# RWKV stage of a two-block transformer kernel: the state's products of y move into the scan over chunks, and the 128-row products follow behind it

## The chip, the cores and the metric

The program runs on one core of a Trainium2 chip. The metric is device time in microseconds (us) of one launch, all weights read from HBM. TensorE (PE) multiplies matrices into PSUM, VectorE (DVE) and ScalarE (ACT) read PSUM and write SBUF, GpSimd (POOL) and SyncE (SP) here mostly issue DMAs. The engines run side by side and are ordered by semaphores alone.

## The reference, cut to what matters

The first block has a mixer with two halves, an attention and an RWKV-7 layer, and a conv FFN; the second block (two layers) follows. The change is inside the RWKV layer, whose core is a scan over the 512 tokens, for 8 heads of 64 channels:

```
def step(state, inp):                       # state: heads x 64 x 64
    sa = einsum('bhvk,bhk->bhv', state, a_t)
    state = state * w_t + sa[..., None] * b_t + v_t[..., None] * k_t
    return state, einsum('bhvk,bhk->bhv', state, r_t)   # y_t
```

The kernel computes it in 8 chunks of 64 tokens. Within a chunk everything is a triangular matrix product; between chunks only the 64x64 state is handed on. For a chunk c, y is a sum of three products: the state at the chunk's start by r (the *state's product*), the corrected values U by the masked scores of b and r (the TR product), and v by the masked scores of k and r (the MR product).

## The kernel before, in words

The work stands in this order: input norm, projections of the mixer, the attention, the RWKV projections, then the RWKV stage (about 390 to 728 us of the span), the merge of both halves (L2017), the output product, and then the FFNs and the second block, which are long rows of 128x128 by 128x512 products in split precision (L1598 to L1600) and fill the other three quarters of the span.

The RWKV stage treats the 8 heads in 4 pairs (p = 0 to 3). Head hb = 0 of a pair sits on partitions 0 to 63, head hb = 1 on 64 to 127, so a slice hd of 64 partitions picks a head. A tile t (of 4) is 128 tokens, that is two chunks. The order on each engine is written out by hand: the lists RW_PE, RW_ACT and RW_DVE (L78 to L106) name every step, each step increments its engine's semaphore once, and `took(p, name)` and `made(p, name)` on TensorE wait for a ScalarE or a VectorE step of that name. Steps with a "+" belong to the next pair and are laid between those of this pair.

For one pair TensorE does: scores (L1846), five levels of a triangular inversion (L1937, L1943, L1948, with ScalarE and VectorE between them), MV, U0 and WT (L1957, L1962, L1966), then the scan over the 8 chunks (L1971 to L1988). In chunk c it multiplies WT with the state Sh[c] (step u, L1977); VectorE adds U0 and writes U (L1356); TensorE adds the chunk's two contributions to the new state in PSUM (L1983, which needs no wait, and L1987, behind U); VectorE scales and adds them into Sh[c+1] (L1362), which the next chunk's u waits for. After the scan comes step y (L1989 to L2001): it waits for the last U, and then for each head and each tile t writes the TR product (L1995), the MR product (L1996) and two state's products (L1999, one for each chunk of 64 tokens) into bank 7 of PSUM, one head's four tiles after the other's. ScalarE copies bank 7 to tA (L760); TensorE transposes the next pair's A (tokA, L1898) meanwhile, and then forms the mean of y (L2004), and the rest of the pair's normalization and the next pair's scores follow. Sh keeps the states of all 8 chunks in SBUF, and AR (or a stage slot for odd pairs) keeps r.

Every operand in this stage is 32-bit float, and each product written in the code is two MATMUL and two LDWEIGHTS in the trace. In the trace's rows a shape such as 128*64 is the rows and columns of the PE array that the product uses: the TR and MR products use all 128 rows and 64 columns (columns 0 to 63 for head 0, 64 to 127 for head 1), the state's products use a quadrant, 64 rows and 64 columns.

Of the kernel before, what the change touches and what calls it, by code (L numbers as in the profile page):

```python
# [23 lines left out]
P = 128  # L24
S = 512
TT = S // P
# [10 lines left out]
HD = 64  # L37
# [6 lines left out]
CHUNK = 64  # L44
# [73 lines left out]
def upto(steps, name):  # L118

    return steps.index(name) + 1  # L120
# [29 lines left out]
def build(nc, A, out, first_block=True, second_block=True):  # L150
# [3 lines left out]
    with ExitStack() as ctx:  # L154
# [46 lines left out]
        psum = ctx.enter_context(nc.psum_tensor("psum", [P, 8, S], F32))  # L201
# [81 lines left out]
        if first_block:  # L283
# [34 lines left out]
            ARs = [AR[:], odd_ar.rearrange("p (t a n) -> p t a n", t=TT, a=2)]  # L318
# [1269 lines left out]
        def _(pe):  # L1588
# [90 lines left out]
            for k in range(KD):  # L1679
# [3 lines left out]
                for tt in range(TT):  # L1683
                    m = pe.transpose(psum[:, k % 4, tt * P:(tt + 1) * P], x_tok[:, tt, k * P:(k + 1) * P], ident)
# [4 lines left out]
            if first_block:  # L1689
# [13 lines left out]
                def made(name):  # L1703
                    pe.wait_ge(ns_dve, upto(NS_DVE, name))
# [25 lines left out]
                for n in range(6):  # L1730
                    took(f"sq{n}")
                    for t in range(TT):
                        c = 8 + 8 * n + 2 * t
                        last = pe.matmul(psum[:, 7, c:c + 2], raw_n[:, n % 2, t * P:(t + 1) * P], head_of,
                                         start=True, stop=True)
# [10 lines left out]
                for n in range(6):  # L1746
# [4 lines left out]
                    for t in range(TT):  # L1751
                        last = pe.transpose(psum[:, 4 + n % 2, t * P:(t + 1) * P], rexp_n[:, n % 2, t], ident)
# [12 lines left out]
                for j in range(TT):  # L1765
                    for h in range(NSA_HEADS):
                        rows = slice(HD * (h % 2), HD * (h % 2) + HD)
                        c = 32 * (h // 2)
                        last = pe.matmul(psum[:, 2 * j + h % 2, c:c + NC], q_n[rows, h // 2, j * P:(j + 1) * P],
                                         kcd[rows, h // 4, 0:NC], start=True, stop=True)  # L1770
# [22 lines left out]
                for m in range(M + 2):  # L1793
                    if m < M:
# [4 lines left out]
                        for c in range(2):  # L1799
                            last = pe.matmul(psum[:, 2 * (m % 2) + c, 0:(j + 1) * P], q_n[rows, h // 2, j * P:(j + 1) * P],  # L1800
                                             kd[rows, c, h // 4, 0:(j + 1) * P], start=True, stop=True)
                        last.then_inc(nscore_done, 1)
                    if m >= 2:
# [6 lines left out]
                        for c in range(2):  # L1810
                            for kt in range(j + 1):
                                last = pe.transpose(psum[:, 4 + c, kt * P:(kt + 1) * P],
                                                    Pn[:, g % 2, c, kt * P:(kt + 1) * P], ident)
# [16 lines left out]
                def rw(p, name, last):  # L1830

                    assert RW_PE[rw_count[0]] == (name, p), (name, p, RW_PE[rw_count[0]])
                    rw_count[0] += 1
                    last.then_inc(rw_pe, 1)
# [77 lines left out]
                for p in range(PAIRS):  # L1912
# [42 lines left out]
                    for m in range(8):  # L1955
                        t, hd = m % 4, slice(HD * (m // 4), HD * (m // 4) + HD)
                        last = pe.matmul(psum[:, 0, HD * m:HD * m + HD], MR[:, m, 0:P], tok[:, 3, t, hd], start=True, stop=True)  # L1957
# [3 lines left out]
                    for m in range(8):  # L1961
                        last = pe.matmul(psum[:, 1, HD * m:HD * m + HD], XT[:, m], MV[:, HD * m:HD * m + HD], start=True, stop=True)  # L1962
                    rw(p, "U0", last)
                    for m in range(8):
                        t, hd = m % 4, slice(HD * (m // 4), HD * (m // 4) + HD)
                        last = pe.matmul(psum[hd, 2, t * P:(t + 1) * P], tok[:, 0, t, hd], XT[:, m], start=True, stop=True)  # L1966
# [3 lines left out]
                    Ut = Ap[:, 4:8].rearrange("p m n -> p (m n)").rearrange("p (h t d) -> p h t d", h=2, t=TT)  # L1970
                    for c in range(NCH):  # L1971
                        t, q = c // 2, slice(CHUNK * (c % 2), CHUNK * (c % 2) + CHUNK)
                        if c >= 1:
                            made(p, f"S{c - 1}")
                        for hb in range(2):
                            hd = slice(HD * hb, HD * hb + HD)
                            last = pe.matmul(psum[q, 3 + hb, 0:HD], WT[hd, CHUNK * c:CHUNK * c + CHUNK], Sh[hd, c],  # L1977
                                             start=True, stop=True)
                        rw(p, f"u{c}", last)
                        if c < NCH - 1:  # L1980
                            for hb in range(2):
                                hd = slice(HD * hb, HD * hb + HD)
                                pe.matmul(psum[hd, 5 + c % 2, 0:HD], tok[q, 2, t, hd], tok[q, 3, t, hd], start=True, stop=False)  # L1983
                            made(p, f"U{c}")
                            for hb in range(2):
                                hd = slice(HD * hb, HD * hb + HD)
                                last = pe.matmul(psum[hd, 5 + c % 2, 0:HD], tok[q, 1, t, hd], Ut[q, hb, t], start=False, stop=True)  # L1987
                            rw(p, f"s{c}", last)  # L1988
                    made(p, f"U{NCH - 1}")  # L1989
                    for hb in range(2):  # L1990
                        hd = slice(HD * hb, HD * hb + HD)
                        for t in range(TT):
                            m = 4 * hb + t
                            dst = psum[hd, 7, t * P:(t + 1) * P]
                            pe.matmul(dst, Ut[:, hb, t], TR[:, m, P:2 * P], start=True, stop=False)  # L1995
                            pe.matmul(dst, tok[:, 3, t, hd], MR[:, m, P:2 * P], start=False, stop=False)  # L1996
                            for q in range(2):
                                part = psum[hd, 7, t * P + CHUNK * q:t * P + CHUNK * q + CHUNK]
                                last = pe.matmul(part, Sh[hd, 2 * t + q], ARs[p % 2][hd, t, 1, CHUNK * q:CHUNK * q + CHUNK],  # L1999
                                                 start=False, stop=q == 1)  # L2000
                    rw(p, "y", last)  # L2001
                    head(p + 1, "tokA")
                    took(p, "y")
# [3 lines left out]
                    for t in range(TT):  # L2007
                        last = pe.matmul(psum[:, 1, 2 * t:2 * t + 2], tB[:, t * P:(t + 1) * P], head_of, start=True, stop=True)
# [3 lines left out]
                    for t in range(TT):  # L2012
                        last = pe.transpose(psum[:, 1, t * P:(t + 1) * P], X[:, t], ident)
# [34 lines left out]
            if second_block:  # L2048
# [25 lines left out]
                for n in range(25):  # L2074
# [7 lines left out]
                    if n >= 1:  # L2082
                        m = n - 1
# [5 lines left out]
                        if m < 8:  # L2089
                            for tt in range(TT):  # L2090
                                last = pe.transpose(psum[:, 4 + m % 2, tt * P:(tt + 1) * P],
                                                    raw[:, m % 2, tt * P:(tt + 1) * P], ident)
                        else:
                            last = pe.matmul(psum[:, 4 + m % 2, :], perm, raw[:, m % 2], start=True, stop=True)
# [17 lines left out]
                for m in range(M + 2):  # L2112
                    if m < M:
# [3 lines left out]
                        for c in range(2):  # L2117
                            rows = slice(HD * c, HD * c + HD)
                            last = pe.matmul(psum[:, 2 * (m % 2) + c, :], q_t[rows, h, j * P:(j + 1) * P],
                                             k_t[rows, h, :], start=True, stop=True)  # L2120
                        last.then_inc(score_done, 1)
                    if m >= 2:
# [4 lines left out]
                        for kt in range(TT):  # L2127
                            last = pe.transpose(psum[:, 4 + g % 2, kt * P:(kt + 1) * P],
                                                E[:, g % 2, 0, kt * P:(kt + 1) * P], ident)
# [5 lines left out]
                for h in range(DIFF_HEADS):  # L2135
                    pe.wait_ge(osq_done, h + 1)
                    for tt in range(TT):
                        last = pe.matmul(psum[:, 4, 4 * h + tt:4 * h + tt + 1], norm_t[:, h % 2, tt * P:(tt + 1) * P],
                                         ones[:, 0:1], start=True, stop=True)
                    last.then_inc(ossq_done, 1)  # L2140
                for h in range(DIFF_HEADS):
# [3 lines left out]
                    for tt in range(TT):  # L2145
                        last = pe.transpose(psum[:, 5 + h % 2, tt * P:(tt + 1) * P], rexp[:, h % 2, tt], ident)
# [10 lines left out]
            for k in range(KD):  # L2157
# [3 lines left out]
                for tt in range(TT):  # L2161
                    m = pe.transpose(psum[:, k % 4, tt * P:(tt + 1) * P], y_out[:, k % 2, tt * P:(tt + 1) * P], ident)
# [120 lines left out]
```

## Time and profile before

| | us |
|---|---|
| runs (3) | 3217.89, 3223.37, 3224.57; median 3223.37 |
| span of the profiled execution, first to last instruction | 3221.2 |
| TensorE busy in it | 3039.4 (94%) |
| VectorE busy | 1522.2 (47%) |
| ScalarE busy | 980.2 (30%) |
| mean granted TensorE clock | 0.938 |

The page states no time of the profiled execution but its span; the median of the runs is 2.2 us above it. Busy time is the time in which at least one of an engine's instructions was under way. The granted clock is TensorE's clock as a share of 2.4 GHz; it takes two values, 1.00 and 0.50 (1.2 GHz), and a figure between them is a mean over a stretch.

### The profile page before, as it was taken

To read this page: it belongs to the slowest core of one execution; us is meant where nothing else is said; L and a number is where in the kernel's file an instruction comes from. 1 tells how busy PE (TensorE), PEld (TensorE's weight loads), DVE (VectorE), ACT (ScalarE), POOL (GpSimd) and SP (SyncE) were. 2 spreads that over 40 slices of the span, in tenths; PEclk is the share of its full clock that TensorE was granted. 3 is DMA by queue.
4 is the path that set the end of the run, shared out by engine and by line. 5 is a ranking of instruction groups with operands and counts; after the bars stand their busy time and mean duration, and the time that the engine had idled before them with its cause. 6 is when DMAs were issued, how large, how long until landed. Compare 5 with 4: busy or idle time off the path is not lost.

```text
span 3221.2 us, 36308 instructions
## 1 busy us (share of the span) xinstructions
PE 3039.4 (94%) x13935; PEld 2401.9 (75%) x13935; DVE 1522.2 (47%) x2198; ACT 980.2 (30%) x1520; POOL 88.2 (3%) x159
## 2 busy tenths in 40 slices
PE   7989888889999999999988999999999999999998
PEld 6844667767878878788866888878887763778887
DVE  4355744426667754555435333243322469343322
ACT  3344333323333322322223222232222216332222
POOL 0000000001100000001100000000000000000000
PEclk9679977779999999999997999999999999899999
DMA  6101400006632346455622333323323220123331
GB/s 216 52 1 44 149 1 1 1 1 200 221 110 96 96 125 189 147 192 188 193 73 73 94 97 93 91 85 98 95 87 99 79 79 1 40 85 98 96 90 63
DMA packets 89888, 309.15 MB, mean 96 GB/s; under 512 B 10288, under 2 KB 14000, under 8 KB 89648
## 3 DMA queue, kind: packets, MB, share of 16 engines
q1 hardware_dynamic: 69040, 232.07, 23.0%
q0 software_dynamic: 20736, 75.51, 7.5%
q8 instruction: 80, 1.31, 0.2%
q14 instruction: 32, 0.26, 0.0%
HBM read 305.44 MB, written 2.10 MB: 95 GB/s over the span
## 4 chain that ended last, share of the span: by engine, by line
PE 88%; DVE 8%; ACT 2%; issue 1%; DMA 0%; SPq 0%; DVEq 0%; ACTq 0%
PE psum L1598 23%; PE psum L1600 23%; PE psum L1599 23%; PE psum L1606 2%; PE psum L1800 1%; PE psum L1937 1%; PE psum L1943 1%; PE psum L1788 1%; PE psum L1740 1%; PE psum L1650 1%; PE psum L1646 1%; PE psum L1647 1%; DVE nmax L1533 1%; PE psum L1995 1%; PE psum L1999 1%
## 5 line engine op out<-in xcount | busy, mean ns | idle before, releaser
L897 DVE TENSOR_TENSOR w_lo<-stage,w_hi 128x1024 fp32r<-128x1024 f32 (+3 forms) x445 | 519.5, 1168 | 896.3 <-ACT w_hi L494 894.9
L1598 PE MATMUL psum<-h_hi,w_hi 128*128 128x512 f32 x2248 | 887.7, 395 | 13.9 <-POOL h_lo L479 10.1
L1600 PE MATMUL psum<-h_hi,w_lo 128*128 128x512 f32 x2248 | 879.0, 391 | 0.0
L1599 PE MATMUL psum<-h_lo,w_hi 128*128 128x512 f32 x2248 | 878.9, 391 | 0.0
L494 ACT ACTIVATE w_hi<-stage 128x1024 fp32r<-128x1024 f32 (+3 forms) x445 | 450.3, 1012 | 1332.9 <-PE psum L1600 1309.3
L1598 PEld LDWEIGHTS psum<-h_hi,w_hi 128*128 128x128 f32 x2248 | 423.9, 189 | 108.2 <-POOL h_lo L479 10.5
L1599 PEld LDWEIGHTS psum<-h_lo,w_hi 128*128 128x128 f32 x2248 | 424.0, 189 | 91.3 <-issue 3.4
L1600 PEld LDWEIGHTS psum<-h_hi,w_lo 128*128 128x128 f32 x2248 | 423.7, 188 | 89.8
L1598 PE MATMUL psum<-hid_hi,w_hi 128*128 128x512 f32 x880 | 351.3, 399 | 6.5 <-DVE hid L984 6.5
L1599 PE MATMUL psum<-hid_lo,w_hi 128*128 128x512 f32 x880 | 348.3, 396 | 0.0
L1600 PE MATMUL psum<-hid_hi,w_lo 128*128 128x512 f32 x880 | 348.2, 396 | 0.0
L1598 PEld LDWEIGHTS psum<-hid_hi,w_hi 128*128 128x128 f32 x880 | 165.5, 188 | 47.6 <-DVE hid L984 8.7
L1600 PEld LDWEIGHTS psum<-hid_hi,w_lo 128*128 128x128 f32 x880 | 165.2, 188 | 40.5
L1599 PEld LDWEIGHTS psum<-hid_lo,w_hi 128*128 128x128 f32 x880 | 165.5, 188 | 38.8
L984 DVE TENSOR_TENSOR hid<-s_buf,psum 128x512 f32<-128x512 f32 x88 | 60.5, 688 | 266.5 <-PE psum L1600 264.9
L935 DVE CUSTOM_DVE_ANT_0 mod_w<-mod_w,c_act 128x1024 f32<-128x1024 f32 x144 | 175.6, 1219 | 0.0
L469 POOL DMA_DIRECT2D mod_w<-in_mod_w x144 | 76.3, 530 | 1544.3 <-DVE modv L935 1367.1
L542 ACT ACTIVATE hid_hi<-hid 128x512 f32 (+1 forms) x110 | 67.9, 618 | 54.8 <-DVE hid L984 54.8
L503 ACT ACTIVATE norm_t<-xT 128x512 f32<-128x512 f32 x64 | 40.3, 630 | 133.1 <-DVE xT L1008 122.7
L1606 PEld LDWEIGHTS psum<-cst,norm_t 128*128 128x128 f32 x512 | 71.8, 209 | 11.1 <-ACT norm_t L503 6.7
L991 DVE TENSOR_TENSOR hid_lo<-hid,hid_hi 128x512 f32 (+1 forms) x110 | 75.3, 685 | 0.0
L1606 PE MATMUL psum<-cst,norm_t 128*128 128x1 f32 x512 | 67.4, 255 | 6.1 <-ACT norm_t L503 6.1
(363 smaller groups left out, 2842.8 us busy)
## 6 DMA issues: line engine op xcount, KB each, us to landing
stage<-in_up SPq DMA_DIRECT2D x220, 512.0 KB, 3.5
mod_w<-in_mod_w POOLq DMA_DIRECT2D x144, 512.0 KB, 4.1
stage<-in_down SPq DMA_DIRECT2D x80, 448.0 KB, 3.3
stage<-in_down SPq DMA_DIRECT2D x40, 512.0 KB, 3.6
stage<-in_w_in SPq DMA_DIRECT2D x24, 512.0 KB, 4.4
stage<-in_w_qkv SPq DMA_DIRECT2D x24, 512.0 KB, 3.5
stage<-in_w_merge SPq DMA_DIRECT2D x16, 512.0 KB, 4.5
PTn<-in_cmp_w SPq DMA_DIRECT2D x1, 4096.0 KB, 12.1
```

Of the source, the lines that this page charges most:

```text
L469: pool.dma_start(mod_w[:, e], A["mod_w"][bass.ds(t + e, 1)].rearrange("a p n -> (a p) n")).then_inc(mod_in[e], 16)
L494: act.activation(w_hi[:, c % 2, 0:kt * cols], stage[:, c % NSTAGE, 0:kt * cols], ACT.Copy).then_inc(hi_done, 1)
L503: act.activation(sq(n_norm, k), xT[:, k], ACT.Square).then_inc(sq_done, 1)
L542: act.activation(hid_hi[:, bass.ds(2 * i + q, 1), :].rearrange("p a n -> p (a n)"), hid[:, q], ACT.Copy).then_inc(hidhi_done, 1)
L897: dve.tensor_tensor(w_lo[:, c % 2, 0:kt * cols], stage[:, c % NSTAGE, 0:kt * cols], w_hi[:, c % 2, 0:kt * cols].bitcast(F32), ALU.subtract ...
L935: dve.tensor_tensor_reduce(out=mod_w[:, t % 2], in0=mod_w[:, t % 2], in1=c_act[:], scale=1.0, scalar=0.0, op0=ALU.mult, op1=ALU.add, accum ...
L984: dve.tensor_tensor(hid[:, q], s_buf[:, q], taps[:, 1] if f == 0 else bank(s.tile + 2 * q + 1), ALU.mult).then_inc(hid_done, 1)
L991: dve.tensor_tensor(hid_lo[:, tile, :].rearrange("p a n -> p (a n)"), hid[:, q], hid_hi[:, tile, :].rearrange("p a n -> p (a n)").bitcast( ...
L1598: pe.matmul(dst, wh[:, n], a_hi[:, k], start=start and n == 0, stop=False)
L1599: pe.matmul(dst, wh[:, n], a_lo[:, k], start=False, stop=False)
L1600: m = pe.matmul(dst, wl[:, n], a_hi[:, k], start=False, stop=stop and n == kt - 1)
L1606: m = pe.matmul(psum[:, 4, tt:tt + 1], sq(n_norm, k)[:, tt * P:(tt + 1) * P], ones[:, 0:1], start=(k == 0 and tt == 0), stop=(k == KD - 1) ...
```

## The change

The state's product of chunk c is issued inside the scan, behind that chunk's contributions to the state, both heads one after the other. It is the first to write bank 7 (`start` only for c = 0). Behind the scan only the MR and TR products are left; they run over the tiles outside and the heads inside, the MR product first, and add to what the scan left. Waits, steps and the semaphore of step y are the same in number and name, and so is the count of products.

```
@@ after step s{c}, in the loop over c
+                        for hb in range(2):
+                            hd = slice(HD * hb, HD * hb + HD)
+                            pe.matmul(psum[hd, 7, CHUNK * c:CHUNK * c + CHUNK], Sh[hd, c],
+                                      ARs[p % 2][hd, t, 1, CHUNK * (c % 2):CHUNK * (c % 2) + CHUNK], start=c == 0, stop=False,
+                                      skip_group_check=True)
                     made(p, f"U{NCH - 1}")
-                    for hb in range(2):
-                        hd = slice(HD * hb, HD * hb + HD)
-                        for t in range(TT):
-                            m = 4 * hb + t
+                    for t in range(TT):
+                        for hb in range(2):
+                            m, hd = 4 * hb + t, slice(HD * hb, HD * hb + HD)
                             dst = psum[hd, 7, t * P:(t + 1) * P]
-                            pe.matmul(dst, Ut[:, hb, t], TR[:, m, P:2 * P], start=True, stop=False)
-                            pe.matmul(dst, tok[:, 3, t, hd], MR[:, m, P:2 * P], start=False, stop=False)
-                            for q in range(2):
-                                part = psum[hd, 7, t * P + CHUNK * q:t * P + CHUNK * q + CHUNK]
-                                last = pe.matmul(part, Sh[hd, 2 * t + q], ARs[p % 2][hd, t, 1, CHUNK * q:CHUNK * q + CHUNK],
-                                                 start=False, stop=q == 1)
+                            pe.matmul(dst, tok[:, 3, t, hd], MR[:, m, P:2 * P], start=False, stop=False,
+                                      skip_group_check=True)
+                            last = pe.matmul(dst, Ut[:, hb, t], TR[:, m, P:2 * P], start=False, stop=t == TT - 1,
+                                             skip_group_check=True)
                     rw(p, "y", last)
```

## Rows read from the trace of the kernel before

**Rows 1.** The page: busy time of the engines, and the chain that ended last.

```profile
PE 3039.4 (94%) x13935; PEld 2401.9 (75%) x13935; DVE 1522.2 (47%) x2198; ACT 980.2 (30%) x1520; POOL 88.2 (3%) x159
...
PE 88%; DVE 8%; ACT 2%; issue 1%; DMA 0%; SPq 0%; DVEq 0%; ACTq 0%
```

**Rows 2.** The chain of 380 to 760 us, summed by line.

```profile
by line: PE psum L1937 10.5%; PE psum L1943 8.3%; PE psum L1995 5.3%; PE psum L1999 5.2%; PE psum L1977 4.1%; PE psum L1846 4.0%; PE psum L1987 3.6%; PE psum L1996 3.6%; issue 3.5%; PE psum L1598 3.3%; DVE XT L1340 3.3%; PE psum L1599 3.3%;
```

**Rows 3.** Timeline: start us, length us, engine, line, tile, count [idle before, releaser]; pair 0.

```profile
466.76 0.48 PE L1977 MATMUL psum<-Sh,Ap 64*64 64x64 f32 x4 [0.46 <-DVE Sh L1362]
...
467.63 0.69 PE L1995 MATMUL psum<-TR,Ap 128*64 128x128 f32 x2 [0.39 <-DVE Ap L1356]
...
468.11 0.63 PE L1996 MATMUL psum<-MR,tok 128*64 128x128 f32 x2
468.67 0.50 PEld L1999 LDWEIGHTS psum<-AR,Sh 64*64 64x64 f32 x4 [0.33 <-issue]
...
469.29 0.69 PE L1995 MATMUL psum<-TR,Ap 128*64 128x128 f32 x2
...
480.30 0.69 PE L1999 MATMUL psum<-AR,Sh 64*64 64x64 f32 x4
480.91 1.11 PE L1898 MATMUL psum<-cst,stage 128*128 128x128 f32 x4
```

**Rows 4.** Timeline of pair 3: the first and the last products of step y.

```profile
705.48 0.69 PE L1995 MATMUL psum<-TR,Ap 128*64 128x128 f32 x2 [0.39 <-DVE Ap L1356]
...
718.15 0.69 PE L1999 MATMUL psum<-stage,Sh 64*64 64x64 f32 x4
```

**Rows 5.** Windows: stretch, its length, PE busy (instructions), granted clock, DMA share, GB/s.

```profile
467.60:481.00 13.40, 13.37 (x65) 0.50 0.00 0
481.00:484.40 3.40, 3.40 (x11) 0.50 0.00 0
484.40:528.70 44.30, 41.31 (x298) 1.00 0.01 1
...
560.90:562.90 2.00, 2.00 (x7) 0.50 0.00 0
...
640.80:644.80 4.00, 4.00 (x14) 0.50 0.00 0
...
658.50:685.70 27.20, 24.57 (x202) 1.00 0.01 1
...
728.00:733.60 5.60, 5.54 (x13) 0.50 0.52 151
```

**Rows 6.** The same products grouped by line over 380 to 760 us: busy, mean ns.

```profile
L1996 PE MATMUL psum<-MR,tok 128*64 128x128 f32 x64 | 20.3, 421 | 0.0
```

**Rows 7.** Timeline of step WT in pair 3: whole, at 688.95, and at 689.80 us.

```profile
688.35 2.88 PE L1966 MATMUL psum<-XT,tok 128*64 128x128 f32 x16
...
688.62 0.63 PE L1966 MATMUL psum<-XT,tok 128*64 128x128 f32 x2
...
689.47 0.70 PE L1966 MATMUL psum<-XT,tok 128*64 128x128 f32 x4
```

**Rows 8.** Timeline of the scan: a chunk's end at the low clock, and one at the full clock.

```profile
465.82 0.48 PE L1987 MATMUL psum<-Ap,tok 64*64 64x64 f32 x4 [0.17 <-DVE Ap L1356]
466.42 0.28 DVE L1362 SCALAR_TENSOR_TENSOR Sh<-psum,Dc,SD 128x64 f32<-128x64 f32 x1 [0.65 <-PE psum L1987]
...
455.41 0.33 PE L1987 MATMUL psum<-Ap,tok 64*64 64x64 f32 x4 [0.27 <-DVE Ap L1356]
...
456.21 0.27 PE L1977 MATMUL psum<-Sh,Ap 64*64 64x64 f32 x2 [0.47 <-DVE Sh L1362]
```

**Rows 9.** Timeline of pair 3's first inversion level: sixteen products at either clock.

```profile
656.02 3.19 PE L1937 MATMUL psum<-X,TR 128*128 128x128 f32 x16
659.04 2.01 PE L1943 MATMUL psum<-XT,Ap 128*128 128x128 f32 x16
```

## The prediction

> **What bounds the kernel now.** I read the page first: TensorE is busy 94% of the span and holds 88% of the chain that ended last [rows 1]; no DMA stands on that chain. So a gain has to come from TensorE's time in the RWKV stage or from the waits on it there. I then asked for the chain over 380 to 760 us alone. The three lines of step y (L1995, L1999, L1996) hold 5.3, 5.2 and 3.6% of these 380 us, 14.1% or 53.6 us together [rows 2]: over 13 us for each of the four pairs, all of it on the path. The lines of the scan (L1977, L1987) are on it too, but as links of a chain with VectorE, not as full work.
>
> The timeline shows why step y is so long. In pair 0 its first product starts at 467.63 and the next step's (tokA) at 480.91: 13.28 us, in eight groups of 1.66 (467.63 to 469.29), each one head and one tile [rows 3]. In pair 3 it runs from 705.48 to 718.84 [rows 4]; pairs 1 and 2 have the same pattern. Inside a group, four MATMULs with 128 rows take from 467.63 to 468.67, and four with 64 rows from 468.67 to 469.29. In the first of these the weight load of L1999 stands idle for 0.33 us with nothing that it waited for in the profile [rows 3]: the array changes from 128 rows to 64 and back, eight times. All of this runs with the granted clock at 0.50, that is 1.2 GHz, in all four pairs (the first row of the windows; the other three are alike) [rows 5]: the clock falls near the start of the scan, whose products are sparse, and does not come back during y, though PE is recorded busy for all of its 13.3 us.
>
> Two things are wasted here, then: the changes between tile shapes, and half of the array's columns, since one head's products use columns 0 to 63 alone and the other head's come only after them.
>
> **The change part by part.**
>
> *The products behind the scan.* 16 products are left, 32 MATMULs, all 128*64, 16 for each half of the columns. Of one half, start follows start by 0.21 us at this clock: the L1996 row has two in 0.63 us of 0.421 us each [rows 3, 6]; I take 0.213, which is what four of them with the next head's start (467.63 to 468.67, less the change) allow. The question is whether the two halves run side by side. Step WT answers it: it issues 16 such MATMULs, eight for columns 0 to 63 and then eight for 64 to 127. In single file at 0.213 they would take 15 x 0.213 + 0.42 = 3.62 us; they took 2.88. At 688.95 two are in flight, which is what one half alone has (0.42 against 0.213), and at 689.80 there are four [rows 7]. So the halves overlap without slowing each other. Counted back from the end (2.88 less 0.42, seven steps of 0.213 and 0.055 for the first after a change), the ninth MATMUL starts 0.91 us in, when the fifth of the first half does: three of the first half were still waiting, and the ninth went past them. In the new order the heads alternate in blocks of four (MR twice, TR twice), so never more than three of one half stand between those of the other, and both halves should run all the time. Then 16 starts a half: 0.055 + 15 x 0.213 = 3.25 us to the last start, and 0.35 us (468.32, the last L1996 start, to 468.67) for the change to the next shape. Step y takes 3.60 us in place of 13.28, a saving of 9.68; in pair 3, counted to the end of the last product, 3.25 + 0.42 = 3.67 against 13.36, or 9.69. Four pairs: 38.7 us. The bounds of this term: full overlap, 3.60; no overlap at all, 31 x 0.213 + 0.055 + 0.35 = 7.01. I take 3.60, as nearest to the row of WT, the only row of this shape with both halves.
>
> The Trainium skill speaks against this value. Its page "TensorE: Matmul & The Clock Gate", Part 3, section "What overlaps and what doesn't", says that MATMULs start and end strictly in program order and only weight loads are pulled ahead. By that rule only the first of each block could start beside the last of the block before. This trace does not agree: 15 steps in program order with one overlap could not end in 2.88 us. I keep it as a rival below.
>
> *The products moved into the scan.* Each of the 8 chunks of a pair gets two products, four MATMULs of 64*64, on two different quadrants of the array, the same tile shape as everything else in the scan, so no change of shape there. They need Sh[c], which u{c} already waited for; r is there since the pair's head; no wait is added. In TensorE's queue they stand behind s{c} and ahead of u{c+1}, which waits for S{c} on VectorE, and VectorE works from s{c}'s end to 466.70. Four MATMULs on one quadrant take 0.62 us (468.67 to 469.29), hence two at most 0.31. s{c}'s last product ends at 465.82 + 0.48 = 466.30, the added ones at 466.61, and u{c+1} starts at 466.76 [rows 8, 3]: covered with 0.15 us to spare. At the full clock: 455.41 + 0.33 = 455.74, at most 456.05, against 456.21: 0.16 to spare. s{c}'s semaphore comes before them, so VectorE isn't delayed. In the last chunk they stand ahead of the wait for U: L1977 ends at 467.24, plus 0.31 is 467.55, against 467.63. So I cost this part at nothing. If the cover failed, the price is bounded by a whole L1999 group with both changes of shape, 468.32 to 469.29 = 0.97 us, less the 0.25 us between the end of VectorE's last need and the restart, or 0.7 us for each of the 28 gaps ahead of a u: 20 us. Below, it can gain: a denser scan might hold the full clock longer, and a chunk takes 1.5 us at the full clock and 1.8 at the low one; at most 0.3 x 28 = 8 us.
>
> *What follows.* tokA, the copy on ScalarE and the mean depend on y alone, and stand idle or queued until it comes (ScalarE's copy waited 29.3 us for L1999's last product). VectorE's only work beside y is the copy L1311, 0.69 us, done by 468.3, before the new y ends at about 471.3. So everything behind moves up by the full amount. DMAs: none is issued in the scan or in y; the weights of the merge wait for the last pair's result, and move up with it; POOL's loads wait for VectorE's own steps in the merge. Instructions are as many as before.
>
> *The clock.* After y the granted clock came back within 3.4, 2.0 and 4.0 us in pairs 0 to 2 [rows 5], while the 128*128 products of tokA and the mean ran. If the denser y brings it back at once, half of the 9.4 us, 4.7 us, is the most to be had; if it comes some 3 us later in each pair, as much is lost. I take 1 us of gain, as both halves of the array now work.
>
> *Sum.* 3221.2 - 38.7 - 1.0 = 3181.5 us of span, and with the 2.2 us by which the median of the runs stands above this span, 3183.7: about 3184 us.
>
> **The rivals.**
>
> *A, program order holds (the skill's rule, as a mechanism here).* Each block of four overlaps its neighbour by one start only: 24 steps in place of 15, 0.055 + 24 x 0.213 + 0.35 = 5.52 us for y. Saving 7.76 a pair, 31.0 in all: 3192 us. For it: the lookahead past three waiting MATMULs is my inference from one step. Against it: rows 7.
>
> *B, no overlap.* The two heads write the same PSUM bank in turns, and could be kept apart: 7.01 us for y, saving 6.27 a pair, 25.1 in all: 3198 us. Against it: WT's two halves also write one bank (bank 2).
>
> *C, the added products are not hidden.* 0.3 to 0.7 us for 28 gaps, 8 to 20 us: 3192 to 3204. Against it: the margins above, and that L1983's products already stand in the same kind of place without a wait.
>
> *D, the clock gives more.* The scan stays at the full clock longer, or y brings it back: 3 to 10 us more, 3174 to 3181.
>
> *E, slower: the clock does not come back.* Dense work ahead of tokA is now 3.6 us where it was 13.3. If that long run of y was what prepared the return, the next pair's inversion runs at 0.50. Its place is the stretches at 1.00 after pairs 0, 1 and 2: 41.31, 41.31 (562.9 to 607.2, like the first) and 24.57 us of PE busy [rows 5]; its price 59% of them, as 16 products took 3.19 us where they take 2.01 [rows 9]: 63 us, which gives 3247. It decides from 38.7 / 63 = 61% of these stretches on. Against it: the clock stayed at 0.50 through all of y's 13.3 us, and in pair 3, where little follows y, it came back only 5.6 us into the merge, in the last of the windows [rows 5]. So what follows y brings it back, and that is unchanged.
>
> *F, step y is not what it seems:* some other step would be late and take most of the saving. I find none; the chain runs through y in all four pairs.
>
> **How the numbers follow.** My forecast 0.66, A 0.10, B 0.06, C 0.06, D 0.08, E 0.03, F 0.01. Faster or slower by 0.2%, 6.4 us, is about what a measurement of this kernel can tell from no change. Faster then holds 0.96, the same 0.01 (F), slower 0.03 (E). The range takes in D below and A, B and most of C above, and 3 us for the spread of the runs: 3173 to 3202.
>
> **What would show it.** In the trace after: step y of each pair takes 3.6 us (5.5 for A, 7.0 for B) from the first L1996-like product to tokA; four products in flight during nearly all of it; no idle of the weight loads inside it; the scan's chunks still 1.8 us apart at the low clock with idle before u{c+1} still put down to VectorE, but some 0.2 us shorter; the pairs' distance down by 9.7 us from 79 us or so. The prediction is wrong if chunks are longer than 1.8 us, if the two halves don't overlap, or if stretches after y that were at 1.00 are at 0.50.

## The result and the profile after

The changed kernel takes 3169.93 us (median of 4 runs, 3167.63 to 3173.15), the kernel before 3223.18; the ratio is 0.9841, with a 95% interval of 0.9827 to 0.9855. That is 53.3 us less where 39.7 were forecast, and below the low end of the range, 3173. The profiled execution has a span of 3165.9 us, 55.3 less than before's, and a mean granted clock of 0.946 in place of 0.938. Three later series of the same kernel gave 3173.8, 3173.5 and 3171.6 against 3223.4, 3220.9 and 3220.3 beside them: 47.3 to 49.6 us less. So the first series stands a few us on the favourable side, and the 8 to 10 us by which these three exceed the 39.7 are still to be explained.

The page after, to compare with [rows 1] (columns as there):

```profile
PE 2991.7 (94%) x13935; PEld 2369.6 (75%) x13935; DVE 1522.0 (48%) x2198; ACT 980.3 (31%) x1520; POOL 88.4 (3%) x159
...
PE 88%; DVE 8%; ACT 2%; issue 1%; DMA 0%; SPq 0%; DVEq 0%; ACTq 0%
```

TensorE lost 47.7 us of busy time with exactly as many instructions, and its weight loads lost 32.3; VectorE, ScalarE and GpSimd kept theirs within 0.2 us. The timeline of step y in pair 0, to compare with [rows 3]; line 1999 is now the MR product, 2001 the TR product, 2006 the mean:

```profile
463.36 0.70 PE L1999 MATMUL psum<-MR,tok 128*64 128x128 f32 x4 [0.18 <-DVE Ap L1356]
463.84 0.65 PE L2001 MATMUL psum<-TR,Ap 128*64 128x128 f32 x4
464.26 0.69 PE L1999 MATMUL psum<-MR,tok 128*64 128x128 f32 x4
...
465.97 0.53 PE L1999 MATMUL psum<-MR,tok 128*64 128x128 f32 x4
466.31 0.41 PE L2001 MATMUL psum<-TR,Ap 128*64 128x128 f32 x4
466.65 0.66 PE L1898 MATMUL psum<-cst,stage 128*128 128x128 f32 x4
```

Each row has four MATMULs, two of each head, and the next row starts some 0.43 us later: two steps of 0.213 for four MATMULs. 13.28 us have become 3.29; the last rows are shorter still because the full clock is back before y ends. In pair 1, where it comes back with tokA, y starts at 530.67 and tokA at 534.34, 3.67 us; pair 3 is the counterpart of [rows 4]:

```profile
663.35 0.70 PE L1999 MATMUL psum<-MR,tok 128*64 128x128 f32 x4 [0.18 <-DVE Ap L1356]
...
666.40 0.69 PE L2001 MATMUL psum<-TR,Ap 128*64 128x128 f32 x4
```

663.35 to 667.09 is 3.74 us, where [rows 4] have 13.36. The windows show the clock; they answer to [rows 5], with the same columns:

```profile
463.30:466.20 2.90, 2.85 (x27) 0.50 0.00 0
466.20:476.00 9.80, 9.70 (x62) 1.00 0.01 2
530.70:534.40 3.70, 3.70 (x33) 0.50 0.00 0
534.50:544.00 9.50, 9.44 (x54) 1.00 0.00 0
...
601.10:602.70 1.60, 1.60 (x5) 0.50 0.00 0
...
667.60:671.00 3.40, 1.78 (x8) 1.00 0.00 0
671.00:674.80 3.80, 1.76 (x9) 0.50 0.02 4
674.80:677.80 3.00, 3.00 (x7) 0.50 0.05 16
```

After y the clock used to stay low for another 3.4, 2.0 and 4.0 us; now it is back 0.5 us before y's end, at it, and 1.6 us behind. Even in pair 3 it comes back once, before the sparse tail lowers it again, and the merge runs 3.0 us at the low clock, not 5.6. This is one trace; pair 3 went otherwise in one of the three repetitions (experiment 1). The scan, at the low clock, one chunk (the counterpart of [rows 8]; line 1991 is the state's product):

```profile
459.75 0.37 PE L1987 MATMUL psum<-Ap,tok 64*64 64x64 f32 x2 [0.18 <-DVE Ap L1356]
459.77 0.37 PE L1991 MATMUL psum<-AR,Sh 64*64 64x64 f32 x1
...
459.93 0.52 PE L1991 MATMUL psum<-AR,Sh 64*64 64x64 f32 x3
460.35 0.28 DVE L1362 SCALAR_TENSOR_TENSOR Sh<-psum,Dc,SD 128x64 f32<-128x64 f32 x1 [0.65 <-PE psum L1987]
...
460.69 0.37 PE L1977 MATMUL psum<-Sh,Ap 64*64 64x64 f32 x2 [0.24 <-DVE Sh L1362]
```

The added products end at 460.45, u starts at 460.69, and VectorE's wait for L1987 is 0.65 us as it was: the chunk keeps its 1.80 us.

To place the rest I cut the RWKV stage of each trace at the same instructions of ScalarE and VectorE: a pair's first L743, L756 (MV), L1347 (WT), the end of the last L1356 (last U), L760 (y), and the next pair's L743 or the first product of the merge. In us, summed over the four pairs, with the traces of the experiments that repeat a kernel. "Exchanged" is the first experiment below; it has before's step y and before's time.

| stretch | before | exchanged | changed, four traces |
|---|---|---|---|
| start to pair 0 | 416.7 | 416.8 | 412.3, 416.4, 411.7, 413.5 |
| inversion, to MV | 123.6 | 122.5 | 122.5, 124.0, 123.9, 122.5 |
| MV to WT | 25.9 | 25.7 | 22.4, 22.6, 24.9, 22.4 |
| scan | 56.1 | 56.2 | 55.3, 55.2, 54.8, 55.3 |
| step y | 53.8 | 53.8 | 15.0, 14.5, 14.9, 15.0 |
| behind y | 52.1 | 52.0 | 47.4, 47.6, 48.5, 47.4 |
| merge to the end | 2493.1 | 2491.5 | 2491.1, 2492.4, 2492.6, 2490.9 |
| span | 3221.2 | 3218.3 | 3165.9, 3172.7, 3171.3, 3167.0 |

Between the means of the two columns before and the four after: step y 38.9, behind y 4.3, MV to WT 2.7, scan 1.0, inversion -0.2, the start 3.3 and the end 0.5; together 50.5. The 3.3 of the start lie ahead of anything that was changed, which leaves 47.2.

The same traces show when the clock came back. With the old step y (before, exchanged, and the kernel of experiment 9) it did so 1.8 to 4.3 us after ScalarE had begun to copy y, in all nine cases of pairs 0 to 2, and in pair 3 only in the merge, 14.7 to 15.0 us after. In the four traces of the changed kernel it came between 0.7 us ahead of that copy and 1.7 us behind it in 15 of 16 pairs, which is 2.7 to 5.4 us after the first product of y. In the sixteenth, pair 3 of the third trace, it came 14.8 us after, as in the kernel before.

### The profile page after: what moved, and what is told of

Same layout as the page of the kernel before. It is cut to its first block, busy times and chain, and to the rows that moved or that the text cites. A ratio compares the mean times of both kernels' runs of the same rounds, so it can differ in the third digit from the quotient of the medians.

```text
span 3165.9 us, 36308 instructions
## 1 busy us (share of the span) xinstructions
PE 2991.7 (94%) x13935; PEld 2369.6 (75%) x13935; DVE 1522.0 (48%) x2198; ACT 980.3 (31%) x1520; POOL 88.4 (3%) x159
## 4 chain that ended last, share of the span: by engine, by line
PE 88%; DVE 8%; ACT 2%; issue 1%; DMA 0%; SPq 0%; DVEq 0%; ACTq 0%
PE psum L1598 24%; PE psum L1599 23%; PE psum L1600 23%; PE psum L1606 2%; PE psum L1800 1%; PE psum L1937 1%; PE psum L1943 1%; PE psum L1788 1%; PE psum L1740 1%; PE psum L1650 1%; DVE nmax L1533 1%; DVE norm_t L918 1%; DVE h_lo L922 1%; PE psum L1647 1%; PE psum L1646 1%
## 5 line engine op out<-in xcount | busy, mean ns | idle before, releaser
L1598 PEld LDWEIGHTS psum<-hid_hi,w_hi 128*128 128x128 f32 x880 | 165.8, 188 | 47.7 <-DVE hid L984 8.6
L1599 PEld LDWEIGHTS psum<-hid_lo,w_hi 128*128 128x128 f32 x880 | 165.8, 188 | 38.9
L542 ACT ACTIVATE hid_hi<-hid 128x512 f32 (+1 forms) x110 | 67.9, 617 | 54.8 <-DVE hid L984 54.8
```

Of the source, the lines that this page charges most:

```text
L542: act.activation(hid_hi[:, bass.ds(2 * i + q, 1), :].rearrange("p a n -> p (a n)"), hid[:, q], ACT.Copy).then_inc(hidhi_done, 1)
L1598: pe.matmul(dst, wh[:, n], a_hi[:, k], start=start and n == 0, stop=False)
L1599: pe.matmul(dst, wh[:, n], a_lo[:, k], start=False, stop=False)
```

## The experiments

Each was run against the kernel before; the ratios have 95% intervals.

**1. The same kernel again**, three times.

> The changed kernel once more, for a second trace. My theory now: of the 53 us, 39 come from step y itself (13.4 us to 3.5 to 3.8 in each pair) and the rest from the granted clock, which comes back at the end of y and not 2 to 4 us later, and which falls later ahead of and in the scan. The part of step y is fixed: 3.4 to 3.9 us again in each pair. The rival holds that the extra 14 us are chance, that is the place of the clock's changes and of the 4.4 us by which the first trace was ahead before the RWKV stage began: then they differ freely in this trace, and the front may be 0 or 4 us ahead. Time under the theory 3167 to 3174.

3173.8 us, 0.9852 (0.9836 to 0.9869). Step y, and what stands behind it, came again. The start did not: 416.4 where the first trace had 412.3. So the 4.4 us by which the first trace led the kernel before, ahead of any changed instruction, were chance.

> The changed kernel a third time, beside the three that follow. Two traces of it had the sum of the four stretches from y's end to the next pair's inversion at 47.4 and 47.6 us (52.1 before), and the four stretches from MV to WT at 22.4 and 22.6 (25.9 before). If both are made by the change, they come again within 0.5 us. If the second is chance of where the clock's changes fall, it lies between 22 and 26. The front (up to the first level of pair 0) between 412 and 418. Time 3169 to 3175.

3173.5 us, 0.9854 (0.9839 to 0.9869). Behind y 48.5, which is 1 us from the other two and not 0.5; MV to WT 24.9; the start 411.7. Pair 3 has 9.19 us behind y, as in the kernel before: here the clock stayed at 0.50 from y until 5.6 us into the merge.

> The changed kernel a fourth time, on the chip of the three before, to compare the two warm kernels with it: 3169 to 3175. Step y 3.4 to 3.9 us a pair, the stretches behind y 47 to 49 us in all, MV to WT between 22 and 25.

3171.6 us, 0.9854 (0.9839 to 0.9869), all stretches as expected.

**2. The kernel before with only the loops exchanged.**

```
-                    for hb in range(2):
-                        hd = slice(HD * hb, HD * hb + HD)
-                        for t in range(TT):
-                            m = 4 * hb + t
+                    for t in range(TT):
+                        for hb in range(2):
+                            hd = slice(HD * hb, HD * hb + HD)
+                            m = 4 * hb + t
```

> The kernel before with the loops of step y exchanged (tiles outside, heads inside), the state's products still between the 128-row ones. If the changes between 128 and 64 rows empty the array, the heads cannot overlap across them, and the eight groups of 1.66 us stay: y 13.4 us, time as before, 3218 to 3225. The rival, that alternating the heads is what brings the gain, expects groups that overlap: y 7 to 9 us, time some 18 to 25 us less.

3220.0 us, 0.9997 (0.9987 to 1.0007): no change. The timeline of pair 1, with the heads in turns:

```profile
552.02 0.69 PE L1995 MATMUL psum<-TR,Ap 128*64 128x128 f32 x2
552.50 0.64 PE L1996 MATMUL psum<-MR,tok 128*64 128x128 f32 x2
553.06 0.69 PE L1999 MATMUL psum<-stage,Sh 64*64 64x64 f32 x4
553.68 0.69 PE L1995 MATMUL psum<-TR,Ap 128*64 128x128 f32 x2
```

Groups of 1.66 us as in [rows 3], two MATMULs in a row and never four: across a change between 128 and 64 rows nothing overlaps. Alternating the heads is worth nothing until the 64-row products are out from between them. The clock in this trace: step y of pair 1, whose last product gives way to tokA at 562.0, then what follows it:

```profile
548.70:562.00 13.30, 13.30 (x65) 0.50 0.00 1
562.00:565.30 3.30, 3.30 (x11) 0.50 0.00 0
565.30:575.00 9.70, 9.70 (x57) 1.00 0.00 0
```

**3. The state's products in one block behind the scan.**

```
-                        for hb in range(2):          # in the scan
-                            ...
                     made(p, f"U{NCH - 1}")
+                    for c in range(NCH):
+                        for hb in range(2):
+                            hd, t = slice(HD * hb, HD * hb + HD), c // 2
+                            pe.matmul(psum[hd, 7, CHUNK * c:CHUNK * c + CHUNK], Sh[hd, c], ...
```

> The changed kernel with the state's products taken out of the scan and put in one block behind it, ahead of the 128-row ones. Sixteen starts a quadrant of 0.107 us are 1.7 us, one change of shape 0.3, then 3.6: y about 5.7 us where it is 3.5 to 3.8, so 8 us more than the changed kernel in all, 3176 to 3180, if the scan hides its products and their being there does nothing for the clock. If the denser scan holds the clock, this kernel loses that too: 4 us more, about 3182 or over, with the clock falling earlier in the scan. If the added products cost the scan time, this kernel is less than 8 us behind, with shorter chunks.

3181.9 us, 0.9876 (0.9860 to 0.9893), 8.1 us over the changed kernel on the same chip (3173.8). In pair 1, all of it at the low clock:

```profile
537.19 0.48 PE L1977 MATMUL psum<-Sh,Ap 64*64 64x64 f32 x4 [0.46 <-DVE Sh L1362]
538.06 1.97 PE L1993 MATMUL psum<-stage,Sh 64*64 64x64 f32 x32 [0.39 <-DVE Ap L1356]
539.97 0.70 PE L2000 MATMUL psum<-MR,tok 128*64 128x128 f32 x4
```

The block takes 1.91 us (538.06 to 539.97), one change of shape included. The scan took 55.5 us, against 54.8 to 55.3 with the products in it: they cost it nothing. So grouping by shape and taking the heads in turns, with nothing moved into the scan, gives 41.5 of the 49.6 us of this chip, and moving the group into the scan 8.1. The time is 1.9 us above the range that I had given for hidden products, at the number of the other theory, in which the denser scan holds the clock; but the scan is not longer here, and that theory does not hold. In the traces step y is 5.4 us longer than in the changed kernel and MV to WT 1.3; the rest of the 8.1 is not placed.

**4. Heads outside behind the scan.**

```
-                    for t in range(TT):
-                        for hb in range(2):
+                    for hb in range(2):
+                        for t in range(TT):
```

> The changed kernel with heads outside and tiles inside behind the scan: sixteen 128*64 products' MATMULs for columns 0 to 63, then sixteen for 64 to 127. With a lookahead past three waiting MATMULs the second half begins with the 13th of the first: 27 steps of 0.213, y about 6.3 us. In strict program order 30 steps, 6.9 us. Without any gain from two column halves at once, 3.7 us, as in the changed kernel. So 10 us more than the changed kernel (13 in program order): 3180 to 3183. If it is the density of both column halves that brings the clock back at y's end, it comes later here and costs up to 4 us more: 3184 to 3187.

3181.9 us, 0.9872 (0.9855 to 0.9889), 8.1 over the changed kernel; in the traces 6.0 of it is step y and some 2 the stretch from MV to WT. Pair 1, where y starts at 539.54:

```profile
541.73 0.63 PE L2001 MATMUL psum<-TR,Ap 128*64 128x128 f32 x2
542.16 0.69 PE L1999 MATMUL psum<-MR,tok 128*64 128x128 f32 x4
542.58 0.69 PE L2001 MATMUL psum<-TR,Ap 128*64 128x128 f32 x4
543.07 0.63 PE L1999 MATMUL psum<-MR,tok 128*64 128x128 f32 x2
```

From 542.16 on there are four in flight for a short while, then two again: the second head has begun. 539.54 + 0.055 + 12 x 0.213 is 542.15, so it begins with the 13th of the first head's 16, three of which still wait. That is the lookahead that I had inferred from WT in [rows 7], to the step. y takes 5.67 us here and not 6.3, as the clock comes back at 544.2, during y. So with half of the columns at a time, but without changes of shape, the clock comes back during y as well: behind y the four stretches sum to 47.2.

**5. Two more copies of the state's products in each chunk.**

```
+                        for e in range(4):
+                            hd = slice(HD * (e % 2), HD * (e % 2) + HD)
+                            pe.matmul(psum[hd, 0, 0:CHUNK], Sh[hd, c], ARs[p % 2][hd, t, 1, 0:CHUNK], ...
```

> The changed kernel with two more copies of the state's products of each chunk behind them in the scan, into a bank that nobody reads. The idle time ahead of u is 0.24 us at the low clock, and each copy takes two starts of 0.107 us a quadrant, 0.21. If the cover theory holds and the clock stays low, each of the 28 gaps grows by 0.42 - 0.24 = 0.2 us or somewhat more, chunks 2.0 us in place of 1.8, in all 4 to 8 us more than the changed kernel: 3176 to 3181. If a denser scan holds the full clock, chunks are 1.5 to 1.6 us and the kernel is 3 to 8 us faster than the changed one: 3163 to 3169.

3173.2 us, 0.9844 (0.9829 to 0.9859): both theories missed. The scan of pair 1 as a whole, and two chunks in it (L1996 are the copies):

```profile
522.50:536.30 13.80, 12.35 (x184) 0.50 0.01 2
...
532.99 0.73 PE L1996 MATMUL psum<-stage,Sh 64*64 64x64 f32 x7
533.53 0.37 PE L1977 MATMUL psum<-Sh,Ap 64*64 64x64 f32 x2
...
534.83 0.68 PE L1996 MATMUL psum<-stage,Sh 64*64 64x64 f32 x7
535.33 0.37 PE L1977 MATMUL psum<-Sh,Ap 64*64 64x64 f32 x2
```

u still starts every 1.80 us: the copies end after it has begun (533.72 against 533.53), so it need not wait until they have ended. My cover of 0.15 us was far too careful. The clock stays at 0.50 although PE is recorded busy for 12.35 of 13.80 us.

**6. A product on each of the two idle quadrants.**

```
+                        for hb in range(2):
+                            hd, other = slice(HD * hb, HD * hb + HD), slice(HD * (1 - hb), HD * (1 - hb) + HD)
+                            pe.matmul(psum[other, 0, 0:CHUNK], Sh[hd, c], ARs[p % 2][hd, t, 1, 0:CHUNK], ...
```

> The changed kernel with one more product a head and chunk on the two quadrants that the state's product leaves free, into a bank that nobody reads. They run beside it, so chunks keep their 1.80 us at the low clock and the time is that of the changed kernel, within 2 us. If the density of all four quadrants is what the clock asks for, it falls later in the scan or not at all: scan 12 us a pair in place of 13.7 to 14.2, and up to 7 us off in all.

3173.2 us, 0.9850 (0.9835 to 0.9865); scan 55.1. They cost nothing and did nothing for the clock.

**7. The MR products ahead of the scan.** They follow WT, in its tile shape, and are first to write bank 7.

```
                     rw(p, "WT", last)
+                    for t in range(TT):
+                        for hb in range(2):
+                            m, hd = 4 * hb + t, slice(HD * hb, HD * hb + HD)
+                            pe.matmul(psum[hd, 7, t * P:(t + 1) * P], tok[:, 3, t, hd], MR[:, m, P:2 * P], start=t == 0, ...
                     made(p, "WT")
```

> The changed kernel with the MR products moved from behind the scan to just behind WT, into the same bank, with the same tile shape as WT. Behind the scan 8 starts a half of the columns are left: y 3.8 - 1.7 = 2.1 us. Ahead of the scan 1.7 us of products are added where TensorE waits 0.85 us for the copy of WT by VectorE and then works on the scan; so the net gain is 0.85 us a pair if VectorE's wait for WT is released before them, 3.4 us in all: 0.1% less than the changed kernel, 3166 to 3171. The rival: the products overlap WT's second half in time and cost less than 1.7, so that up to 1.7 us a pair, 6.8 in all, is gained. If the clock then comes back later, as y is only 2.1 us of dense work, up to 4 us are lost again.

3172.9 us, 0.9849 (0.9836 to 0.9863), the same as the changed kernel (3173.5), and not the 3166 to 3171 that I had given. y fell to 2.08 us in every pair, 8.3 in all, a gain of 6.5. But the four stretches behind y took 49.9 us, 2.2 more than the mean of the changed kernel, and MV to WT 28.0, 4.9 more. Of these 4.9, 1.2 arose in pair 0, where the clock fell at 451.3, before the first product that this edit moved (456.21): chance, or at least not its doing. What follows y is slower because the clock came back 3.6 to 3.7 us after y's first product in pairs 0 to 2, which is as soon as in the changed kernel but 1.6 to 1.7 us behind so short a y; in pair 3 it stayed low until the merge. Pair 1:

```profile
539.77 1.98 PE L2004 MATMUL psum<-TR,Ap 128*64 128x128 f32 x16 [0.18 <-DVE Ap L1356]
541.68 1.12 PE L1898 MATMUL psum<-cst,AR 128*128 128x128 f32 x4
...
541.50:543.40 1.90, 1.90 (x9) 0.50 0.00 0
543.40:550.00 6.60, 6.60 (x43) 1.00 0.00 0
```

**8. Products in the waits around MV, U0 and WT.** In the first kernel two, two and three, in the second three, three and five, into bank 6, which nobody reads there.

```
+                    for _ in range(3):
+                        pe.matmul(psum[0:128, 6, 0:P], pair_ones[:, 0:128], pair_ones, ...
                     made(p, "Y5b")
                     ...
                     rw(p, "MV", last)
+                    for _ in range(3):
+                        pe.matmul(psum[0:128, 6, 0:P], pair_ones[:, 0:128], pair_ones, ...
                     took(p, "MV")
                     ...
                     rw(p, "WT", last)
+                    for _ in range(5):
+                        pe.matmul(psum[0:64, 6, 0:P], pair_ones[:, 0:64], pair_ones, ...
                     made(p, "WT")
```

> The changed kernel with products into a bank that nobody reads, put where TensorE waits around MV, U0 and WT in each pair: two ahead of the wait for the last inversion step, two behind MV, three behind WT. The theory is that the sparse stretch from MV to the scan is what makes the clock fall there, and that it costs about 5 us over the four pairs (22.4 to 24.9 us measured where a pair at the full clock takes 4.3). If the added density holds the clock until the scan, the stretch takes 4.3 to 5 us a pair, 17 to 20 in all, and the kernel is 3 to 6 us faster than the changed one: 3166 to 3170. The rival: the clock falls all the same, the added products then run at half speed and are no longer hidden, and the stretch grows to 26 us or more: 3174 to 3178.

3167.3 us (3163.1 to 3170.7), 0.9840 (0.9826 to 0.9853).

> As the kernel before this one, with three, three and five products. At the full clock these are 0.64, 0.64 and 0.8 to 1.07 us, just under the idle times of 0.8, 0.8 and 1.2. If density is what matters, the clock holds more surely than with the smaller number: 17 to 19 us for the stretch. If products are already in the way, each pair loses 0.3 to 0.7 us against the smaller number.

3165.2 us (3163.2 to 3166.7), 0.9829 (0.9815 to 0.9842). The changed kernel beside them took 3171.6 (3169.2 to 3176.6). MV to WT takes 4.20 to 4.27 us in all eight cases, 17.0 in all for either, and the scan 53.6 and 53.0. The windows from MV to WT, pair 2 of the kernel before and then pair 2 of the second of these:

```profile
606.30:613.30 7.00, 6.24 (x32) 0.57 0.01 2
```

```profile
579.00:584.50 5.50, 5.50 (x55) 1.00 0.00 0
```

With TensorE never idle there, the clock holds until the scan; in all eight cases it fell 3.3 to 6.4 us behind the start of VectorE's copy of WT. The second kernel is the fastest of the study: 6.4 us below the changed kernel on the same chip, with no run of either inside the other's spread, by work that computes nothing. The first is 4.3 us below, and its spread meets that of the changed kernel.

**9. The kernel before, with eight products more ahead of MV in pair 0.**

```
+                    for _ in range(8 if p == 0 else 0):
+                        pe.matmul(psum[:, 6, 0:P], pair_ones, pair_ones, ...
                     made(p, "Y5b")
```

> The kernel before with eight products more (1.7 us at the full clock) ahead of MV in pair 0 alone, into a bank that nobody reads: everything behind stands half a step later against the clock's changes. The stretch from MV to WT took 6.32, 7.00 and 6.70 us in pairs 1 to 3, and 5.85, 6.36 and 6.59 in the kernel with exchanged loops. If its saving in the changed kernel (5.3 to 5.7, 4.3 to 7.2 and 5.8 to 6.7) is chance of where the changes of the clock fall, one of these three moves by over 1 us here, and the sum leaves 18.8 to 20.1. If it comes of the shorter step y, the sum stays between 18.8 and 20.1. y stays 13.4 a pair; time 3219 to 3227.

3217.7 us, 0.9995 (0.9986 to 1.0005). MV to WT took 5.86, 6.34 and 6.57 us in pairs 1 to 3, 18.8 in all: none moved by over 1 us, and the sum is at the edge of what I gave. The edit did not do what it was meant to, either. The eight products lengthened pair 0's inversion by 0.7 us and shortened its stretch from MV to WT from 5.85 to 4.27 us, since the clock now held there. Pair 1 began 0.6 us sooner after pair 0, and not half a step later. So it does not decide between the two theories; what it shows is that such products hold the clock in the kernel before too. The time is 1.3 us below the range given. It starts at 413.4, so the start varies as much in a kernel with before's step y.

## Why the prediction was wrong, point by point

- *Step y, 13.28 to 3.60 us a pair, 38.7 in all:* right. Measured 38.9 between the means, 3.67 us in pair 1 from first start to tokA. Some 0.5 of the 38.9 is the clock's, where it came back before y's end; a y wholly at the low clock takes 3.83 us in the table's stretch, against 13.44. Both halves of its reason hold: no overlap across changes of shape (experiment 2), and a lookahead past three waiting MATMULs (experiment 4). Rival A, program order, would have had 5.5 us a pair; rival B 7.0. Both fall. The rule of program order that the Trainium skill's page "TensorE: Matmul & The Clock Gate" states in Part 3, section "What overlaps and what doesn't", falls with rival A for these products.
- *The added products at nothing:* right, with more room than I gave (experiments 3 and 5). Rival C falls. Its price was set too high besides: the 0.25 us that it takes off stands in no row, and TensorE's idle time ahead of a u is 0.46 us there, which makes 0.5 us a gap and 14 in all.
- *What follows moves up in full:* right; F falls. E falls too: all stretches at 1.00 stayed so.
- *The clock, "I take 1 us of gain":* this is the step that failed, a term of the sum that was mis-sized. Behind y it gave 4.3 us: 3.3 in pairs 0 to 2, of the 4.7 that I had named as the most to be had there, and 1.0 in pair 3, for which I had allowed nothing. I had seen that 13.3 us of recorded business did not raise the clock in the kernel before, and read from it that y does not matter to the clock. The experiments show that it was the broken y that did not: with the changes of shape the clock stayed low through y and beyond in all twelve pairs (before, experiments 2 and 9); without them it was back about y's end in 15 pairs of 16 in the changed kernel, and in all pairs of experiments 3 and 4, where the column halves work at once or one after the other; and with only 2 us of such work it was late again (experiment 7). What in the products makes this difference was not isolated. Rival D, to which I gave 0.08, was what happened in kind; its low end, 3174, still lies above all four medians.
- *Ahead of y:* not in my sum. MV to WT came out 2.7 us shorter and the scan 1.0. That the clock sets the first is shown by experiment 8, where holding it takes the stretch to 17.0 us. Why the changed kernel meets the fall of the clock later in most of pairs 1 to 3 is open. It may follow from the shorter pair, or be chance of where the falls lie: pairs 1 to 3 took 20.0, 18.8 and 18.8 us in three traces with the old y, 16.5, 16.8, 19.0 and 16.5 in the changed kernel, 17.1 and 16.7 in experiments 5 and 6, whose y is as short, and 18.5 and 19.5 in experiments 3 and 4, whose y lies between.
- *Chance:* of the first trace's 55.3 us, 4.4 lie ahead of pair 0, a stretch that took anything from 411.7 to 418.9 us over all kernels. The range was to leave 3 us for the spread of runs, but its low end, 3173, is only 1 us below D's 3174; with the full 3 it would have been 3171. The other three series have medians of 3171.6 to 3173.8, so the first lies 1.7 us or more below all of them, and that much of the miss is luck of the draw; the clock's term is what brought the time to the range's edge.

## What to carry to other kernels

Sort small products by the tile shape they use, and put those of the odd shape where the array already runs in it; only then alternate the column halves, in blocks that the queue can look past (here no more than three waiting). When a change makes a stretch of TensorE denser, price the clock behind it as well: look in the trace at what work the clock came back after, not at the recorded busy share. And where short waits in a chain let the clock fall, unneeded products in those waits can pay (here 6.4 of 3171.6 us).

## What the runs showed of the hardware that was not expected

- Recorded business says little about the clock: it stayed at 0.50 with PE busy 13.30 of 13.30 us (mixed shapes, experiment 2) and 12.35 of 13.80 (64x64 products, experiment 5), and at 1.00 with 41.31 of 44.30 [rows 5].
- MATMULs on different column halves start out of program order: the 17th of a sequence with the 13th, at no cost to either: both halves keep their step of 0.213 us (experiment 4).
- A change between 128 and 64 rows costs 0.35 us from start to start at the low clock where 0.213 is the step, and no product was seen to start across it ahead of its turn; eight such changes and back made 13.3 us of work that takes 5.5 when sorted by shape (experiment 3, pair 1).
- A 64x64 product queued ahead of a waiting one does not delay it by its full length: three times the state's products in each chunk left the chunk at 1.80 us (experiment 5).
